# Where ScalarE and VectorE split a weight chunk, relative to steps that wait for other engines, in a two-block fp32 transformer kernel

## The reference

```
x = first_block(x, ...)    # norm, w_in, MoBA attention (8 heads) + MLA attention (8 heads), gates,
                           # w_branch_a / w_branch_b, w_out, then SwiGLU: w_gate, w_up, w_down; norm
x = second_block(x, ...)   # norm, w_in_2, gated linear attention (4 heads, chunked) + differential
                           # attention (4 heads), w_o_2, norm, then conv feed-forward; norm
```

## Time and profile before

| | |
|---|---|
| median of 3 runs | 2459.6 us (2458.02 to 2459.71) |
| profiled execution | 2457.82 us, of it 2456.1 us from the first to the last instruction |
| PE matmul busy | 2430.6 us, 99% |
| PE weight load busy | 2015.1 us, 82% |
| DVE busy | 1804.5 us, 73% |
| ACT busy | 1370.3 us, 56% |
| POOL busy | 49.6 us, 2% |
| granted TensorE clock | 0.999 of full speed on average |
| DMA | 460.11 MB, 187 GB/s on average |

### The profile page before, as it was taken

How to read it: one execution, slowest core, us unless ns; L and a number is a source line. 1 busy time by engine, 2 the same in 40 slices (tenths; PEclk the granted TensorE clock), 3 DMA queues, 4 the chain that set the end, 5 groups by cost and what they waited for, 6 DMA issues and landing times.

```text
span 2456.1 us, 28978 instructions
## 1 busy us (share of the span) xinstructions
PE 2430.6 (99%) x11187; PEld 2015.1 (82%) x11187; DVE 1804.5 (73%) x2292; ACT 1370.3 (56%) x1726; POOL 49.6 (2%) x96
## 2 busy tenths in 40 slices
PE   9999999999999999999999999999999999999998
PEld 7888888888888888888888778878788888888887
DVE  6455545655688888989778587565789999999854
ACT  6446556445555555556556465554666666667543
POOL 1000010000000000000002100000000000000000
PEclk9999999999999999999999999999999999999999
DMA  7655545666566666666666545556566666665664
GB/s 233 191 171 157 185 146 160 192 201 201 183 201 195 201 197 200 195 187 207 191 212 197 162 146 156 156 171 212 160 203 194 189 204 185 196 195 189 213 204 157
DMA packets 239587, 460.11 MB, mean 187 GB/s; under 512 B 16614, under 2 KB 18832, under 8 KB 239072
## 3 DMA queue, kind: packets, MB, share of 16 engines
q1 hardware_dynamic: 237744, 452.65, 59.8%
q0 software_dynamic: 1680, 5.69, 0.8%
q10 hardware_dynamic: 32, 0.01, 0.0%
HBM read 456.19 MB, written 2.10 MB: 187 GB/s over the span
## 4 chain that ended last, share of the span: by engine, by line
PE 96%; DVE 2%; ACT 2%; issue 1%; DMA 0%; DVEq 0%; POOL 0%; SPq 0%; ACTq 0%; POOLq 0%
PE acc L987 13%; PE acc L989 13%; PE acc L988 13%; PE acc L686 13%; PE acc L688 13%; PE acc L687 13%; PE mis L987 3%; PE mis L989 3%; PE mis L988 3%; PE acc L707 1%; PE acc L705 1%; PE acc L706 1%; PE mis L659 1%; PE mis L1251 1%; PE mis L784 1%
## 5 line engine op out<-in xcount | busy, mean ns | idle before, releaser
L1566 ACT ACTIVATE wf<-wf_raw 128x1024 fp32r<-128x1024 f32 x452 | 471.5, 1057 | 473.4 <-DVE wf_raw L2349 199.0
L1992 DVE TENSOR_TENSOR lo<-raw,hi 128x1024 fp32r<-128x1024 f32 (+1 forms) x405 | 486.9, 1218 | 335.8 <-ACT hi L1306 331.8
L2361 DVE TENSOR_TENSOR wf<-wf_raw,wf 128x1024 fp32r<-128x1024 f32 x452 | 533.5, 1219 | 60.1 <-ACT wf L1566 56.9
L1306 ACT ACTIVATE hi<-raw 128x1024 fp32r<-128x1024 f32 (+1 forms) x405 | 417.2, 1051 | 268.0 <-PE acc L688 207.7
L987 PE MATMUL acc<-wf,xb_hi 128*128 128x512 f32 x874 | 343.1, 393 | 1.2 <-DVE stg L2462 1.2
L989 PE MATMUL acc<-wf,xb_lo 128*128 128x512 f32 x874 | 340.5, 390 | 0.0
L988 PE MATMUL acc<-wf,xb_hi 128*128 128x512 f32 x874 | 340.1, 389 | 0.0
L686 PE MATMUL acc<-hi,xa_hi 128*128 128x512 f32 (+1 forms) x704 | 275.0, 391 | 4.0 <-DVE lo L1992 2.4
L688 PE MATMUL acc<-hi,xa_lo 128*128 128x512 f32 (+1 forms) x704 | 271.7, 386 | 0.0
L687 PE MATMUL acc<-lo,xa_hi 128*128 128x512 f32 (+1 forms) x704 | 271.4, 386 | 0.0
L686 PE MATMUL acc<-hi,xb_hi 128*128 128x512 f32 x608 | 242.4, 399 | 4.4 <-DVE lo L1992 4.4
(11 more groups left out here) (480 smaller groups left out, 3675.2 us busy)
## 6 DMA issues: line engine op xcount, KB each, us to landing
raw<-in_w_in SPq DMA_DIRECT2D x216, 512.0 KB, 4.2
wf_raw<-in_w_ffn_in SPq DMA_DIRECT2D x160, 512.0 KB, 3.7
wf_raw<-in_w_down SPq DMA_DIRECT2D x88, 512.0 KB, 4.2
wf_raw<-in_w_gate SPq DMA_DIRECT2D x80, 512.0 KB, 3.8
wf_raw<-in_w_up SPq DMA_DIRECT2D x80, 512.0 KB, 4.2
wf_raw<-in_w_ffn_out SPq DMA_DIRECT2D x44, 512.0 KB, 3.8
raw<-in_w_ffn_out SPq DMA_DIRECT2D x44, 512.0 KB, 4.9
raw<-in_w_out SPq DMA_DIRECT2D x32, 512.0 KB, 4.7
```

The lines of the kernel that those rows point to most:

```text
L1306: nc.scalar.activation(hi[:, slot, :, 0:width], raw[:, slot, :, 0:width], ACT.Copy)\
L1566: nc.scalar.activation(wf[:, f_slot[c], 0, :, :], wf_raw[:, f_slot[c], 1, :, :], ACT.Copy)\
L1992: V.tensor_tensor(lo[:, slot, :, 0:width], raw[:, slot, :, 0:width], hi[:, slot, :, 0:width].bitcast(F32), ALU.subtract).then_inc(lo_ready, 1)
L2361: V.tensor_tensor(wf[:, f_slot[c], 1, :, :], wf_raw[:, f_slot[c], 1, :, :], wf[:, f_slot[c], 0, :, :].bitcast(F32), ALU.subtract).then_inc ...
```

## The change

It reorders instructions; none is added or removed, and no number of buffers changes. "Hoisted" below means: `split` of a chunk is written ahead of the other steps of the same g.

1. **ckv/uq**: ACT splits chunk 3 ahead of `root`, and DVE ahead of its wait for the root.
2. **gate1**: ACT and DVE split chunks 0 and 1 ahead of the `kvm` evictions, ACT splits chunk 4 ahead of the `qrt`/`krt` copies, and PE's wait for `krt_in` goes from before chunk 3 to before the steps of chunk 4.
3. **GLA**: ACT splits ahead of a head's steps 3, 5 and 6 (`early`); DVE splits at step 4 behind the first four `g_x` instructions, not behind all fourteen.
4. **o2**: at each of the first eight chunks both engines split behind the attention steps and ahead of the strips' work; ACT's silu goes from c = 2 to c = 3.
5. **ffn entry**: DVE writes the two `stg` halves ahead of `lo` of chunk (0,1), not behind.

```diff
@@ PE, gate1
-                pe.wait_ge(krt_in, 1)
...
+                    if j == 0 and c == MLA_FIRST:
+                        pe.wait_ge(krt_in, 1)
                     mla_steps(j * per + c)
@@ ACT, uq, at c == LEAD
+                    split(n, c)
                     root(1, rs_c)
                     side_hi(i0 + 1, ct, 4, gains(V_KV, 2), blocks=2)
...
-                split(n, c)
+                if c != LEAD:
+                    split(n, c)
@@ ACT, gate1
             for c in range(4 * per):
+                if c < 2 or c == MLA_FIRST:
+                    split(n, c)
                 if c < 2:
                     results(Count(PH["ukv"][0]), c + 2)
...
-                split(n, c)
+                if c >= 2 and c != MLA_FIRST:
+                    split(n, c)
@@ ACT, in2b (GLA)
+                    early = any(due(g, GLA_FIRST, GLA_PERIOD, step, GH) is not None for step in (3, 5, 6))
+                    if early:
+                        split(Count(n0), g)
                     gla_steps(g)
...
-                    split(Count(n0), g)
+                    if not early:
+                        split(Count(n0), g)
@@ ACT, last_heads
+                split(Count(PH["o2"][0]), c)
                 if c == 1:
                     side_hi(i4 + 1, xa, 4, gains(V_GLA, 2) * 2, 1)
                     root(7, rs_o[:, 12:16])
-                if c == 2:
+                if c == 3:
                     results(Count(PH["o2"][0]), -1)
                     silu((PH["o2"][1] - 1) % 2, W)
@@ DVE, ffn entry
             f_lo_of(run_b[0], 0, 0)
-            f_lo_of(run_b[0], 0, 1)
...
             V.engine_nop().then_inc(staged, 2)
+            f_lo_of(run_b[0], 0, 1)
             f_lo_of(run_b[0], 1, 0)
```

More of the change, by code:

```diff
@@ L1817, in _ @@
                         nc.scalar.activation(rs_tmp[:, 0:1], ident[:, 0:1], ACT.Sqrt)
-                    split(Count(n0), j * per + c)
+                    if j:
+                        split(Count(n0), j * per + c)
             n5, t5 = n0 + DT * per, t0 + DT - 1
@@ L2228, in _ @@
                 mla_steps(c)
-                split(n, c)
+                if c >= 2:
+                    split(n, c)
             n0, t0, i0, per = PH["branch"]
@@ L2710, in _ @@
                         side_lo(i4, xa, 0, gains(V_DIF, 2) * 2, 1)
-                    split(Count(n0), g)
+                    if due(g, GLA_FIRST, GLA_PERIOD, 4, GH) is None:
+                        split(Count(n0), g)
             def last_heads(c):
                 diff_steps(NB * KD // CK + c)
+                split(Count(PH["o2"][0]), c)
                 if c == 1:
```

## The result

The changed kernel takes 2443.85 us in the median (2443.6 to 2444.14), the kernel before 2459.35 in the same comparison. The ratio is 0.9938, with a 95% interval of 0.9926 to 0.9951: 15.5 us or 0.63% faster. The forecast was 2446.1, its range 2443.1 to 2452.0; the measured time lies inside it, 0.75 above its low end.

The account below looks back on a forecast made before the run. PE, busy 99% of the span, was taken as the bound. Gains of 1.2 (uq), 2.6 (gate1), 5.7 (GLA), 2.8 (o2) and 1.2 (ffn entry) sum to 13.5 us, from 2459.6 to 2446.1; range 2443.1 to 2452.0.

Parts of the forecast that it names:

- What bounds the kernel, and the price of a wait: Whole kernel: PE bounds it, busy 99%; each of 13 listed waits costs its idle plus 0.26 us, together at most 13.9.
- PE's busy time: Whole kernel: PE's busy time should stay at 2430 us while the span falls to 2442.6.
- uq, gate1: ckv/uq and gate1: early splits and the later `krt` wait remove PE's waits there, gaining 1.2 and 2.6 us.
- GLA head 0: First GLA head: the long wait for `lo` 10 goes, a 0.25 remainder stays at chunk 11; gain 2.0 us.
- GLA, heads 1 to 3: Later GLA heads: five waits, from late `lo` behind `g_x` and late `hi` on ACT, go; gain 3.7 us.
- o2: Start of o2: three waits go, the strip is just in time; gain 2.8 us, or 2.3 if it is late.
- ffn entry: First feed-forward's entry: the `stg` wait goes, `lo` is slightly late with 0.25 kept; gain 1.2 us.
- The median: Whole kernel's time: the 13.5 us gain taken from the median of 2459.6 gives 2446.1 us.
- B: Rival at the 13 places: waits change their name, each keeping two thirds of its loss; 2455.0 us, chance 0.06.
- C: Rival behind 1380 us: with pauses gone the granted clock falls, making it slower; 2476 us at 60 us, chance 0.03.
- Rival A: Rival in GLA: the decay chain becomes the new wait, costing 1.2 us per head, 4.8 in four; 2450.9, chance 0.15.

Follow-up runs that it names:

- `krt` alone: Kernel before with only PE's wait for `krt_in` moved from ahead of the first product to chunk 4; 2457.89 us against 2458.99, ratio 0.9994.
- the half changes: Kernel before with one part of an edit: GLA's ACT order 2452.17 us, GLA's DVE order 2458.17, PE's `krt_in` wait 2457.89; before 2458.99.
- DVE's half alone: Kernel before with only DVE's part of the GLA change, `lo` ahead of the remaining `g_x`, ACT's order unchanged; 2458.17 us, ratio 0.9996.

## Why the prediction was right, and where it was not

- **What bounds the kernel, and the price of a wait.** Right. PE's 13 waits were nearly the whole matter (short unlisted pauses add about 0.9), and idle plus 0.26 is what each gave: at o2 three waits gave 2.87 (2.8 forecast), at uq and gate1 3.78 (3.8).
- **PE's busy time.** Wrong by its own step: the forecast kept it at 2430, but the 0.26 per wait lies in busy time (the modelled end, the slow restart), so 13 x 0.26 = 3.4 had to leave it. It fell from 2430.6 to 2427.4, by 3.2.
- **uq, gate1.** Right in both terms. `krt` alone gives 1.39 of the 1.9; the other 0.5 us needs ACT's `hi` of chunk 4 ahead of the copies, which the forecast named.
- **GLA head 0.** Right, 2.17 for 2.0, and so was the remainder, 0.30 for 0.25. The pause itself gave 1.98; the rest is a short unlisted pause two chunks further on (starts 0.28 and 0.34 apart in before, 0.23 and 0.24 in after), which the forecast did not count.
- **GLA, heads 1 to 3.** The mis-sized term: 3.7 forecast, 4.77 measured. Three pauses of 0.14 + 0.11 there, one in each head, are too short for the list and were set aside as "some tenths"; they are 0.75. The rest, 0.3, I can't place in single pauses. The causes were also named too evenly: the forecast spoke of two, and ACT's order alone is all of it.
- **o2.** Right. The strip came in time, and the silu's move, which the forecast counted among the means, did nothing.
- **ffn entry.** Right: 1.15 for 1.2, with a remainder of 0.16 + 0.11 where 0.25 was kept.
- **The median.** The forecast carried the profiled execution's 13.5 over to it. The gain measured is 2.0 larger: 1.24 more between starts, 1.3 in how far each profiled execution lies under its median, less the 0.5 by which after's trace is longer elsewhere. Of the 15.5 measured, 14.2 is the span of the profiled executions; the other 1.3 is that before's was 1.5 under its median and after's 0.25 under. Some of that distance is probably the low clock behind head 0's pause, which the trace of before doesn't show. The forecast had no term for it.
- **Rivals B and C.** B: no wait changed its name in the whole change; it did in two of the half changes. C: the granted clock of after is 0.999, and every stretch of before already had 1.00 in the windows view, so fewer pauses had nothing to lift there. The clock does enter, though not in the traced execution of before, and with the other sign: it was low only behind the longest pauses, and the change takes one of them away.
- **Rival A.** Its condition came true in part. DVE now waits for Exp ahead of its products with `g_qk`, in heads 1 to 3, and 2.43 us for Ln ahead of `g_z` in head 0; before had neither wait. None of these made a listed wait of PE, so the price did not fall due. The row is of DVE's waits in after, from 1376 to 1530:

```profile
DVE g_x L2648 <- ACT g_x L1748: 1.1, 4, 0.5
```

## What to carry to other kernels

The list of waits names the engine that came last, not the one whose order is at fault: follow the chain one engine back, and expect that of two faults in a row the repair of one may show nothing, as DVE's half alone did in head 0. Price a pause of the bounding engine by the distance between starts, and add up the short ones that a list leaves out. Before an instruction is moved, look at which waits stand ahead of its new place.

## What the runs showed of the hardware

- A pause of PE of 2.0 us (three of six traces) or 1.86 us (the one trace that has it) was followed, 0.8 to 1.6 and 0.2 us behind the restart, by some 3 us at a granted clock of 0.50, at a cost of 1.4 to 1.6 us. The pauses of 1.57 us at the second feed-forward's entry (in all but two of the traces), of 1.60 at `krt` and of 1.52 were not followed by it, nor were the pauses of 1.8 us near the kernel's start (in seven traces). So the length of the pause alone does not settle it.
- After a pause the first matmul of 512 columns is shown with 0.47 to 0.50 us instead of 0.39, and the second starts 0.31 to 0.34 behind it instead of 0.23. This holds for a pause of 0.03 us as for one of 2 us, so a pause too short for the list still costs 0.25 to 0.3.
